# Paged attention in a decoder step: pages laid partition-major, later keys by sums within a partition

## What is computed

```python
def stick_breaking(q, k, v, b_sb, q_pos, k_pos):
    scale = q.shape[-1] ** -0.5
    z = jnp.einsum('bthe,bshe->bhts', q, k) * scale + b_sb...
    mask = k_pos[None, :] < q_pos[:, None]
    log_stay = jnp.where(mask, jax.nn.log_sigmoid(-z), 0.0)
    later = lax.cumsum(log_stay, axis=3, reverse=True) - log_stay
    a = jnp.where(mask, jnp.exp(jax.nn.log_sigmoid(z) + later), 0.0)
    return jnp.einsum('bhts,bshe->bthe', a, v)

past_k = pool_k[page_table].reshape(Bd, P, H_C, HEAD_DIM)   # 32 pages of 128 tokens a sequence
past_v = pool_v[page_table].reshape(Bd, P, H_C, HEAD_DIM)
```

## Time and profile before

| | |
|---|---|
| median of 3 runs | 3718.3 us |
| profiled execution | 3721.61 us, span 3720.0 us |
| mean granted TensorE clock | 0.952 |
| busy share: PE, DVE, ACT, POOL | 92%, 55%, 42%, 19% |
| V pages, by GpSimd's queue (q0) | 50.35 MB |
| the changed phase | some 300 of 3720 us, from 1670 on |

### The profile page before, as it was taken

The page is one execution under the profiler, slowest core; times in us unless marked ns, Lnnn a source line. Parts: engine busy times, 40 slices in busy tenths (PEclk is TensorE's granted clock), DMA queues, the critical chain, the costliest instruction groups (busy, mean ns, idle before and its releaser), DMA issues. The chain is left out here.

```text
span 3720.0 us, 61127 instructions
## 1 busy us (share of the span) xinstructions
PE 3405.9 (92%) x21973; PEld 2930.7 (79%) x21973; DVE 2045.5 (55%) x4143; ACT 1557.1 (42%) x3047; POOL 706.7 (19%) x986
## 2 busy tenths in 40 slices
PE   8999999989995999589997968999989999899996
PEld 7999999944443666356665858999989999899996
DVE  2211134468995665436664446656675665756664
ACT  3321122268882444224442225444454443544342
POOL 0111111156771334114440011000010000100000
PEclk9999999989996989789998988999999999999998
DMA  5654456421005541669984552434353444422222
GB/s 202 216 193 164 149 177 194 151 66 43 10 10 117 107 87 41 234 235 331 354 302 145 174 184 93 132 118 155 127 166 122 139 135 142 149 85 77 72 69 77
DMA packets 435826, 533.92 MB, mean 144 GB/s; under 512 B 93749, under 2 KB 370870, under 8 KB 430550
## 3 DMA queue, kind: packets, MB, share of 16 engines
q1 hardware_dynamic: 407214, 416.41, 36.1%
q10 hardware_dynamic: 11946, 63.40, 5.0%
q0 software_dynamic: 16384, 50.35, 3.8%
HBM read 436.28 MB, written 143.91 MB: 156 GB/s over the span
## 5 line engine op out<-in xcount | busy, mean ns | idle before, releaser
L3519 PE MATMUL p_DP<-p_UH,p_WH 128*128 128x352 f32 x1536 | 497.7, 324 | 20.7 <-issue 14.4
L3520 PE MATMUL p_DP<-p_UL,p_WH 128*128 128x352 f32 x1536 | 496.7, 323 | 0.0
L3521 PE MATMUL p_DP<-p_UH,p_WL 128*128 128x352 f32 x1536 | 496.6, 323 | 0.0
L3519 PE MATMUL p_UP<-p_TH,p_WH 128*128 128x352 f32 x1344 | 439.4, 327 | 53.0 <-DVE p_TL L3429 36.9
L3520 PE MATMUL p_UP<-p_TL,p_WH 128*128 128x352 f32 x1344 | 434.1, 323 | 0.0
L3521 PE MATMUL p_UP<-p_TH,p_WL 128*128 128x352 f32 x1344 | 434.0, 323 | 0.0
L916 PE MATMUL p_PP<-p_WH,p_HH 128*128 128x384 f32 (+1 forms) x1224 | 420.1, 343 | 9.2 <-DVE p_WL L618 4.8
L917 PE MATMUL p_PP<-p_WL,p_HH 128*128 128x384 f32 (+1 forms) x1224 | 408.5, 334 | 0.0
L918 PE MATMUL p_PP<-p_WH,p_HL 128*128 128x384 f32 (+1 forms) x1224 | 407.9, 333 | 0.0
L603 ACT ACTIVATE p_PT<-p_PP,p_rs 128x384 f32<-128x384 f32 (+1 forms) x153 | 87.3, 570 | 539.3 <-PE p_PP L918 539.3
L3519 PEld LDWEIGHTS p_DP<-p_UH,p_WH 128*128 128x128 f32 x1536 | 290.9, 189 | 23.0 <-issue 21.8
(11 more groups left out here) (445 smaller groups left out, 6677.9 us busy)
## 6 DMA issues: line engine op xcount, KB each, us to landing
p_WU<-in_w_up SPq DMA_DIRECT2D x48, 1024.0 KB, 5.4
p_WD<-in_w_down SPq DMA_DIRECT2D x192, 256.0 KB, 2.9
cw_K<-in_cache_sb_k SPq DMA_DIRECT2D x192, 192.0 KB, 4.3
cw_V<-in_cache_sb_v POOLq DMA_DIRECT2D x192, 192.0 KB, 5.1
out_s_wk<-in_cache_win_k ACTq DMA_DIRECT2D x64, 382.5 KB, 3.5
out_s_wv<-in_cache_win_v ACTq DMA_DIRECT2D x64, 382.5 KB, 4.2
p_HH<-scratch_xh SPq DMA_DIRECT2D x34, 512.0 KB, 4.8
p_HL<-scratch_xl SPq DMA_DIRECT2D x34, 512.0 KB, 5.5
```

Of the source, the lines that this page charges most:

```text
L3519: pe.matmul(out, hi, rhi, start=first, stop=False, skip_group_check=True)
L3520: pe.matmul(out, hi, rlo, start=False, stop=False, skip_group_check=True)
L3521: return pe.matmul(out, lo, rhi, start=False, stop=last, skip_group_check=True)
```

## The change

A page is laid so that each partition of a tile holds 8 successive tokens. Page i of a quarter goes to partitions i, i + 8, i + 16, ... (16 of them), and each of these takes 8 * 384 numbers, 12288 B, in one run. All 8 slots of a tile are filled by every page, 16 partitions a page. Before, a page was one slot on all 128 partitions.

Token 8p + r of page i is now in partition i + 8p, slot r. So the later keys of the same 8 tokens are in the same partition, and VectorE sums them there: L[r] += L[r+1], from slot 6 down to 0, in place. L[0] is then a partition's total. All other later keys of the quarter lie in other partitions, which come later in the order (page, place in the page); that order is a permutation of the partitions. `nlate` is the triangle of -1 in that order, made at the start by two products of TensorE: `after` (a strict triangle) by the permutation `places`, the result copied by VectorE to `turned_after`, and that by `places` again, copied to `nlate`. The two cumulative products have 48 columns in place of 384: nlate by L[0], and nones by CR, the sum carried from later quarters (CR += L[0] of the quarter before). VectorE subtracts the in-partition sums from ZB and adds the 48 columns, broadcast over the slots, to give AR.

```diff
--- before.py
+++ after.py
@@ -2076,8 +2076,9 @@

     def load(self, eng, dst, src, landed, pages, q):

-        for r in range(self.NP):
-            eng.dma_start(dst[q][:, r, :], src[bass.ds(pages[self.NP - 1 - r], 1), :, :].rearrange("a p c -> p (a c)")).then_inc(landed[q], 16)
+        for i in range(self.NP):
+            page = src[bass.ds(pages[i], 1), :, :].rearrange("a (p r) c -> (a p) (r c)", r=self.NP)
+            eng.dma_start(dst[q][i:P:self.NP, 0:self.NP, :].rearrange("p r c -> p (r c)"), page).then_inc(landed[q], 16)

...
         ZB = [m.sb(f"ZB{i}", [P, NP, C]) for i in range(2)]
         E = m.sb("E", [P, NP, C])
         L = [m.sb(f"L{i}", [P, NP, C]) for i in range(2)]
-        SL = [m.sb(f"SL{i}", [P, NP + 1, C]) for i in range(2)]
+        CR = [m.sb(f"CR{i}", [P, C]) for i in range(2)]
...
         ntri = m.sb("ntri", [P, P])
+        nlate = m.sb("nlate", [P, P])
+        after, places, turned_after = (m.sb(x, [P, P]) for x in ("after", "places", "turned_after"))
+        late_ps, late_ok = m.sem("late_ps"), m.sem("late_ok")
         nones = m.sb("nones", [P, P])
...

         AP_ = APB[:, 0:NP * C].rearrange("p (r c) -> p r c", c=C)
+        LATER = APB[:, 0:C]
...
             pool.affine_select(out=ntri[:, :], in_=ntri[:, :], compare_op=ALU.is_ge, fill=0.0, base=0,
                                pattern=[[-1, P]], channel_multiplier=1).then_inc(consts, 1)

-            pool.wait_ge(consts, 3)
+            pool.affine_select(out=after[:, :], in_=after[:, :], compare_op=ALU.is_gt, fill=0.0, base=0,
+                               pattern=[[-1, P]], channel_multiplier=1).then_inc(consts, 1)
+            place = places[:, :].rearrange("p (x y) -> p x y", y=NP)
+            pool.affine_select(out=place, in_=place, compare_op=ALU.not_equal, fill=1.0, base=0,
+                               pattern=[[-1, P // NP], [-(P // NP), NP]], channel_multiplier=1).then_inc(consts, 1)
...
@@ -2596,7 +2608,8 @@
                 dve.wait_ge(arg_ok, n + 1)
                 if n:
                     dve.wait_ge(a_ok, n)
-                ins = dve.tensor_tensor(AR[:, :, :], ZB[n % 2][:, :, :], AP_[:, :, :], ALU.add)
+                dve.wait_ge(own_ok, n + 1)
+                ins = dve.tensor_tensor(AR[:, :, :], ZB[n % 2][:, :, :], LATER[:, None, :].broadcast_to([P, NP, C]), ALU.add)
...
+            for i, x in enumerate((turned_after, nlate)):
+                dve.wait_ge(late_ps, i + 1)
+                dve.tensor_copy(x[:, :], Z2[i][:, 0:P]).then_inc(late_ok, 1)
             keys(0, 1)
...
@@ -2642,19 +2658,22 @@
                 dve.tensor_scalar(E[:, :, :], ZB[s][:, :, :], 40.0, None, ALU.min).then_inc(zc_ok, 1)
                 if n:
                     exponents(n - 1)
-                src = SI[:, b, :] if q == 0 else SL[1 - s][:, NP, :]
-                dve.tensor_copy(SL[s][:, 0, :], src).then_inc(s_ok, 1)
+                if q == 0:
+                    dve.tensor_copy(CR[s][:, :], SI[:, b, :]).then_inc(s_ok, 1)
+                else:
+                    dve.tensor_tensor(CR[s][:, :], CR[1 - s][:, :], L[1 - s][:, 0, :], ALU.add).then_inc(s_ok, 1)
                 if n + 1 < N:
                     keys(n + 1, 3)
                 dve.wait_ge(sp_ok, n + 1)
                 dve.tensor_tensor(L[s][:, :, :], ZB[s][:, :, :], E[:, :, :], ALU.max).then_inc(l_ok, 1)
                 dve.wait_ge(l_ok, n + 1)
-                for r in range(NP):
-                    dve.wait_ge(s_ok, n * (NP + 1) + r + 1)
-                    dve.tensor_tensor(SL[s][:, r + 1, :], SL[s][:, r, :], L[s][:, r, :], ALU.add).then_inc(s_ok, 1)
-                    if n + 1 < N and r == 4:
+                for i, r in enumerate(reversed(range(NP - 1))):
+                    dve.wait_ge(s_ok, n * NP + i + 1)
+                    dve.tensor_tensor(L[s][:, r, :], L[s][:, r + 1, :], L[s][:, r, :], ALU.add).then_inc(s_ok, 1)
+                    if n + 1 < N and i == 4:
                         keys(n + 1, 5)
-                dve.wait_ge(s_ok, n * (NP + 1) + NP + 1)
+                dve.wait_ge(s_ok, (n + 1) * NP)
+                dve.tensor_tensor(ZB[s][:, :, :], ZB[s][:, :, :], L[s][:, :, :], ALU.subtract).then_inc(own_ok, 1)
                 if q == 0 and b:
...
             def cumulate(n):
-                pe.wait_ge(s_ok, (n + 1) * (NP + 1))
+                pe.wait_ge(s_ok, (n + 1) * NP)
                 pe.wait_ge(yn_ok, 1)
                 if n:
                     pe.wait_ge(ar_ok, n)
                 if folded(n) is not None:
                     fold_out(folded(n))
-                pe.matmul(AP_[:, :, :], ntri[:, :], L[n % 2][:, :, :], start=True, stop=False)
-                pe.matmul(AP_[:, :, :], nones[:, :], SL[n % 2][:, 0:NP, :], start=False, stop=True).then_inc(arg_ok, 1)
+                pe.matmul(LATER, nlate[:, :], L[n % 2][:, 0, :], start=True, stop=False)
+                pe.matmul(LATER, nones[:, :], CR[n % 2][:, :], start=False, stop=True).then_inc(arg_ok, 1)
...
-            pe.wait_ge(consts, 2)
+            pe.wait_ge(consts, 5)
+            pe.matmul(Z2[0][:, 0:P], after[:, :], places[:, :], start=True, stop=True).then_inc(late_ps, 1)
+            pe.wait_ge(late_ok, 1)
+            pe.matmul(Z2[1][:, 0:P], turned_after[:, :], places[:, :], start=True, stop=True).then_inc(late_ps, 1)
             turn(0, (0, 1, 2))
             new_logits()
             turn(0, (3, 4, 5))
```

More of the change, by code:

```diff
@@ L2431, in stick_sample_phase @@
         arg_ok = m.sem("arg_ok")
+        own_ok = m.sem("own_ok")
         ar_ok = m.sem("ar_ok")
@@ L2460, in _ @@
             pool.memset(fold[:, :], 0.0)
+            pool.memset(places[:, :], 0.0)
             pool.memset(maskn[:, :, :], 0.0)
-            for t in (ntri, nones):
+            for t in (ntri, after, nones):
                 ins = pool.memset(t[:, :], -1.0)
@@ L2469, in _ @@
                                pattern=[[-1, P]], channel_multiplier=1).then_inc(consts, 1)
-            pool.wait_ge(consts, 3)
+            pool.affine_select(out=after[:, :], in_=after[:, :], compare_op=ALU.is_gt, fill=0.0, base=0,
[3 more added lines that the diff above has]
+                               pattern=[[-1, P // NP], [-(P // NP), NP]], channel_multiplier=1).then_inc(consts, 1)
+            pool.wait_ge(consts, 5)
             new = maskn[:, :, :].rearrange("p b (h t) -> p b h t", h=2)
@@ L2474, in _ @@
                                pattern=[[-DT, DB], [0, 2], [0, DT]], channel_multiplier=1).then_inc(consts, 1)
-            pool.wait_ge(consts, 4)
+            pool.wait_ge(consts, 6)
             pool.affine_select(out=new, in_=new, compare_op=ALU.is_gt, fill=NEG, base=0,
@@ L2479, in _ @@
             for c in range(P // HW):
-                pool.wait_ge(consts, 5 + c)
+                pool.wait_ge(consts, 7 + c)
                 pool.affine_select(out=fold[:, :], in_=fold[:, :], compare_op=ALU.not_equal, fill=1.0, base=-c * HW,
@@ L2617, in _ @@
             dve.wait_ge(zn_ok, 1)
-            dve.wait_ge(consts, 5)
+            dve.wait_ge(consts, 7)
             for g in range(PAIRS):
@@ L2676, in new_sums @@
             def new_sums():
-                pe.wait_ge(consts, 9)
+                pe.wait_ge(consts, 11)
                 pe.wait_ge(si_ok, 1)
@@ L2720, in back @@
                 pe.wait_ge(zs_ok, 2 * n + half + 1)
+                if n == 0:
+                    pe.wait_ge(late_ok, 2)
                 if n:
```

## The result

The changed kernel takes 3828.6 us, the median of 4 runs (3803.2 to 3857.8), beside 3718.0 us for the kernel before (3716.7 to 3718.4). The ratio is 1.030, with a 95% interval from 1.022 to 1.038. The forecast was 3805 in a range of 3712 to 3850, and slower. The profiled execution took 3818.2 us (span 3816.2), 96.6 us more than that of before. In a second series it took 3811.7 us.

What follows compares the result with a forecast made beforehand. TensorE and the engines around it were taken to set the pace, DMA just keeping up. Slow pages add 89 us, the -4.4 us of arithmetic disappearing in page waits: 3718.3 + 89 = 3807, stated as 3805, range 3712 to 3850.

Steps and rivals of the forecast that it cites:

- The pages: Page loads in the paged-cache phase: every-eighth-partition transfers fall to 240 GB/s, against 362 needed; slow pages given 0.70.
- rival A: Page loads: they move at full rate, so only the arithmetic counts, 3714 us; chance 0.17.
- The sum: Paged-cache phase: 91.2 MB of pages at 240 GB/s to 2055, then a short tail, ending near 2060: +89 us.
- The cumulative products: TensorE's pair of products in each round: 0.41 us instead of 1.32, worth almost nothing in an ordinary round.
- The ordinary round: The 25 rounds without a fold: weights start 0.02 us earlier, held by Ln's end, 0.5 us in all.
- The 7 rounds with a fold: Rounds that also fold a sequence's output, where the products are late: 0.82 us saved each, 5.7 us in all.
- VectorE's subtraction: Added subtraction in each round, 0.55 us apiece: costs nothing under VectorE's idle time; 11 us over 32 rounds without that cover.
- rival C: VectorE becomes late: no slow pages, but the subtraction shows, 11 us less what is saved, about 3725 us; chance 0.05.
- Rival B: TensorE's freed time in the rounds is cashed in: 29 us go, 3689 us; chance 0.03.
- The end: Last round of the phase: one addition less and shorter products, minus 1.1 us.
- The start: Before TensorE's first transposes: waits for five constants and two products with a copy between, plus 2.9 us.
- The granted clock: TensorE's clock in the rounds: if it fell to the lower level while waiting, 8.2 us of work would be 16.

Runs made afterwards that it cites:

- e1: The kernel before with only the changed kernel's page loads (16 partitions, every eighth, 12288 B runs) and the old sums: 3864.0 us, ratio 1.039.
- e2: The changed kernel with the old page loads on 128 partitions, keeping the new sums: 3719.5 us, ratio 0.9996.
- e5: The kernel before with each page loaded to 64 partitions, every second one, in runs of 3072 B: 3725.0 us, ratio 0.999.
- e7: The kernel before with each page loaded to 32 partitions, every fourth one, in runs of 6144 B: 3729.1 us, ratio 1.001.
- e3: The kernel before with each page loaded to 16 adjoining partitions in runs of 12288 B: 4025.8 us (one run).
- e6: The kernel before with each page loaded to 64 adjoining partitions in runs of 3072 B: 3826.8 us, ratio 1.026.

## Why the prediction was right, and where it was off

*The pages* were the deciding term, and that is shown: e1 and e2 split the change, and e5 to e7 show that it is the choice of partitions. I took 240 GB/s from the earlier trace rows; the profile has 244. The step from a load of 64 adjoining partitions to one of every eighth was the risk, which rival A stated ("if what slowed rows 6 was that all 16 engines wrote into 64 adjoining partitions"). e1 excludes it.

*The sum* of +89 us was too small: by 8 in the profiled execution (96.6, of which 2.3 arose ahead of the phase) and by some 20 against the median (110.6). Its last step failed: "Behind the last landing (some 2 us) come the value products and the rest" took the last V page for what the end waits for. The amount and the rate held: 91.2 MB at 244 GB/s from 1676.92 end at 2051, and the engines move 119 GB/s from 2050 to 2055 and then next to nothing. V pages do land last, and nothing waits for them. TensorE's last wait is for a K page; it ends at 2043.56, and the phase's last total stands at 2068.8:

```profile
2043.56 1.97 PE L2724 MATMUL sc_KTP<-sc_ident,sc_KP 128*128 128x128 f32 x8 [4.48 <-DMA sc_KP<-in_cache_sb_k]
```

Behind it come the rest of that round and the whole last one, a tail of 25 us, not 5.5. The rest is scatter: the runs lie between 3803 and 3858, and the rate in the second series' profile was 251.

*The cumulative products*: 0.41 us a pair forecast and found. That they buy almost nothing is shown by e2. The ordinary round gained 0.15 us, not 0.02, because the row's end of Ln was not the bound (above): 22 by 0.15 is 3.3 us, not 0.5. The 7 rounds with a fold gained 0.9 us each, forecast 0.82.

*VectorE's subtraction* was costed at nothing under cover of its idle time, with 0.55 us a piece. In e2 the additions end at 1706.24 (1705.80 + 0.44), the subtraction starts at 1706.28 and lasts 0.56, and the round is shorter than before, so rival C is out. *Rival B*, a round of 7.8 us, is out by e2's 8.53.

*The end* was forecast at -1.1, and e2 shows nothing: from the last round's additions to its value products it takes 4.92 us (1960.49 to 1965.41), before 4.87. There the value products of the round before take 2.68 us instead of 1.52, at a granted clock of 0.60 from 1960 to 1963 behind a stop of 2.05 us, and the cumulative products stand behind them. That slower work was no term of the sum.

*The start*: +2.9 forecast, +3.3 found (4.48 instead of 1.18 us). In all, the sums' arithmetic inside the phase is about -6 in e2's profile (from the first constant to the last total 295.1 us, before 301.0), forecast -4.4. It can't be told in the measured time, which is 0.9996 with an interval of 0.12% to either side.

*The granted clock* fell to 0.91 in the stretch, not to the lower level throughout, so that the upper end of 3850 was not needed for it; one of four runs, 3857.8, lies over the range all the same.

The experiments point to no version that beats both. As they are written, the sums need eight tokens of a page in a partition, and with one DMA a page that is the layout that loads slowly; four tokens a partition (e7) load at the full rate, but the sums' whole worth is within the scatter.

## What to carry to other kernels

Ask of every load which partitions one transfer reaches, not only how many or how long its runs are: here a tile filled by many transfers was not filled at the tile's rate. A stride of up to four partitions kept the full rate here, eight did not. And before a product is made smaller, look at what else arrives at the point that waits for it: some 29 us of TensorE were saved, in e2 that gave 10 us of rounds, and the longer start took 3.3 of them back.

## What the runs showed of the hardware that I had not expected

Fewer, longer runs did not make the issue on SyncE's queue cheaper: 128 rows of 1536 B take 333 ns, 16 rows at every eighth partition 496 ns. GpSimd's issues went from 536 to 481 ns. In e3, 16 adjoining partitions, SyncE's took 316 ns:

```profile
L2081 SPq DMA_DIRECT2D cw_K<-in_cache_sb_k x192: 315/316/1526, 1609.2 to 2189.4; - x192
```

Every second partition (475 ns) and every fourth (473 ns) are dear too, but so are the 64 adjoining ones of e6:

```profile
L2081 SPq DMA_DIRECT2D cw_K<-in_cache_sb_k x192: 468/469/3591, 1612.0 to 2006.6; - x192
```

So the step between the partitions alone does not explain it, nor does the number of rows or their length; what does was not settled. The longer issue cost nothing that shows: e5 and e7 had it and were as fast as the kernel before.
